# First modulation loaded by pairs of features, the gate columns multiplied behind the fourth tile

## What is computed

```python
c_act = silu(c)                                   # one row for the prompt, one for the sample
mod = c_act @ ada_w + ada_b                       # 6 x 1024 columns: sh1, sc1, gt1, sh2, sc2, gt2
hn = rmsnorm(x, norm1_g) * (1 + sc1) + sh1
proj = hn @ w_in                                  # split into pb, pc, ph, q, k, v, z, a, bb, ga, gb
g = -exp(a_log) * softplus(a + dt_bias)           # a, bb: 8 columns each, the gate columns
beta = sigmoid(bb)
# convolutions, gated delta rule, two mixers, residual with gt1, second norm, feed-forward, final norm
```

## Time and profile before

| | us |
|---|---|
| median of 3 runs | 1252.98 (1252.93 to 1253.11) |
| profiled execution | 1251.88 |
| its span, first to last instruction | 1250.2 |
| PE busy | 1225.0 (98%) |
| DVE busy | 670.6 (54%) |
| ACT busy | 449.1 (36%) |
| mean granted PE clock | 0.992 of full |

### The profile page before, as it was taken

The page is one execution under the profiler, slowest core; times in us unless marked ns, Lnnn a source line. Parts: engine busy times, 40 slices in busy tenths (PEclk is TensorE's granted clock), DMA queues, the critical chain, the costliest instruction groups (busy, mean ns, idle before and its releaser), DMA issues.

```text
span 1250.2 us, 27424 instructions
## 1 busy us (share of the span) xinstructions
PE 1225.0 (98%) x11560; PEld 1175.0 (94%) x11560; DVE 670.6 (54%) x904; ACT 449.1 (36%) x798; POOL 117.2 (9%) x255
## 2 busy tenths in 40 slices
PE   6999999999999999999999999999999999999997
PEld 4899999999999999999999999979999999999997
DVE  5586566455464555544967984464543343343334
ACT  4584434223232222324343333363332332232254
POOL 5021111201102011011110001000300000000000
PEclk8999999999999999999999999999999999999999
DMA  9932233212222122144864567422422322222212
GB/s 274 269 89 78 76 86 94 61 52 69 62 68 63 52 84 57 35 111 153 239 199 133 158 207 287 142 61 84 129 75 84 85 85 85 84 83 76 79 52 77
DMA packets 193886, 135.44 MB, mean 108 GB/s; under 512 B 4570, under 2 KB 185276, under 8 KB 192504
## 3 DMA queue, kind: packets, MB, share of 16 engines
q1 hardware_dynamic: 186320, 105.30, 30.0%
q0 software_dynamic: 7008, 28.48, 6.8%
q10 hardware_dynamic: 456, 0.16, 0.1%
HBM read 128.02 MB, written 5.90 MB: 107 GB/s over the span
## 4 chain that ended last, share of the span: by engine, by line
PE 93%; DVE 2%; SPq 2%; ACT 2%; DMA 1%; issue 0%; DVEq 0%; ACTq 0%
PE gp L575 79%; PE dp L779 2%; PE gp L601 2%; PE dp L788 1%; SPq L308 1%; PE dp L844 1%; PE dp L810 1%; PE dp L829 1%; PE dp L837 1%; PE dp L789 1%; PE dp L749 1%; PE dp L816 1%; DMA ada_w<-in_ada_w 1%; SPq L304 1%; PE dp L819 0%
## 5 line engine op out<-in xcount | busy, mean ns | idle before, releaser
L575 PE MATMUL gp<-a_hi,w_hi 128*128 128x288 f32 x1856 | 406.9, 301 | 2.3 <-DVE w_lo L1429 2.3
L575 PE MATMUL gp<-a_hi,w_lo 128*128 128x288 f32 x1856 | 397.3, 296 | 0.0
L575 PE MATMUL gp<-a_lo,w_hi 128*128 128x288 f32 x1856 | 396.9, 295 | 0.0
L575 PEld LDWEIGHTS gp<-a_hi,w_hi 128*128 128x128 f32 x1856 | 296.8, 189 | 13.1 <-issue 4.1
L575 PEld LDWEIGHTS gp<-a_hi,w_lo 128*128 128x128 f32 x1856 | 298.8, 189 | 0.0
L575 PEld LDWEIGHTS gp<-a_lo,w_hi 128*128 128x128 f32 x1856 | 298.3, 188 | 0.0
L1429 DVE TENSOR_TENSOR w_lo<-w_raw,w_hi 128x1024 fp32r<-128x1024 f32 x160 | 196.0, 1225 | 110.3 <-ACT w_hi L1023 109.3
L1184 ACT ACTIVATE xp<-gp 128x576 f32<-128x576 f32 x113 | 73.7, 652 | 452.5 <-PE gp L575 432.4
L1023 ACT ACTIVATE w_hi<-w_raw 128x1024 fp32r<-128x1024 f32 x160 | 168.8, 1055 | 2.3 <-DMA w_raw<-in_w_in 2.2
L575 PE MATMUL gp<-f_hi,w_hi 128*128 128x288 f32 x496 | 106.8, 297 | 0.0
L575 PE MATMUL gp<-f_lo,w_hi 128*128 128x288 f32 x496 | 106.2, 296 | 0.0
(11 more groups left out here) (314 smaller groups left out, 1258.0 us busy)
## 6 DMA issues: line engine op xcount, KB each, us to landing
w_raw<-in_w_in SPq DMA_DIRECT2D x72, 512.0 KB, 3.8
w_raw<-in_w_ff SPq DMA_DIRECT2D x64, 512.0 KB, 4.0
ada_half<-in_ada_w POOLq DMA_DIRECT2D x32, 512.0 KB, 4.6
ada_w<-in_ada_w SPq DMA_DIRECT2D x16, 512.0 KB, 7.5
w_raw<-in_w_a_out SPq DMA_DIRECT2D x8, 512.0 KB, 4.4
w_raw<-in_w_b_out SPq DMA_DIRECT2D x8, 512.0 KB, 4.1
w_raw<-in_w_o SPq DMA_DIRECT2D x8, 512.0 KB, 5.8
fin_vu<-in_final_ada_w POOLq DMA_DIRECT2D x4, 1024.0 KB, 18.6
```

The source lines that it names most:

```text
L575: last = T_.matmul(gp[:, 2 * b + h, 0:HALF], wp[:, b, k, :], ap[:, k, h * HALF:(h + 1) * HALF], start=(k == 0 and wp is w_hi and ap is hi) ...
```

## The change

- The weight of the first modulation comes in four blocks of 2 MB, each for two features: two DMAs of 1024 x 256 in rows of 1 KB. Row product, row copy and turn are made four times instead of eight, with twice the columns.
- The rows of c (c_p, c_s) are turned by themselves ahead of x; c_act is made behind the first x tile. Of the other rows, seven go by SP's queue behind block 0, four by ACT's.
- DVE scales four features before it copies the vectors; it splits the low part of tile 0 between the first pair's sample and low parts.
- PE's order is written out anew: tile 1 no longer runs four features behind tile 0 but close to it at the end.
- PE gets five filler products of ones and x (`keep_busy`): one before and one after row product 0, three behind turn 0.
- The gate columns are loaded last (POOL waits for block 3), high and low part side by side as 128 columns, and multiplied behind tile 3: 32 matmuls instead of 48. DVE adds the two halves. The gates are worked out beside tiles 4 to 7 instead of 0 to 3.

The diff, cut to its core:

```diff
 SP
-        for f in range(KT):
+        def ada_block(q):
             for e in range(2):
-                sp.dma_start(ada0_w[:, f, :, e, :], ada_v[:, :, D * e + f * P:D * e + f * P + P]).then_inc(ada_full[f], 16)
-            if f in (0, 2):
-                load(f // 2, 0, f // 2, wt(w_in, C_QKV + f // 2 * P))
+                sp.dma_start(ada0_w[:, q, :, 2 * P * e:2 * P * e + 2 * P], ada_v[:, :, D * e + 2 * P * q:D * e + 2 * P * q + 2 * P])\
+                    .then_inc(ada_full[q], 16)
+        ada_block(0)
+        row("ada_b", ...); row("cache_a", ...); row("conv_a_w", ...); row("final_g", ...)
+        row("out_g", ...); row("pad", ...); row("final_b", ...)
+        load(0, 0, 0, wt(w_in, C_QKV))
+        ada_block(1)
+        load(1, 0, 1, wt(w_in, C_QKV + P))
+        ada_block(2)
+        ada_block(3)
 POOL, behind its masks
+        pool.wait_ge(ada_full[3], 32)
+        ... the four DMAs of the gate columns and biases, moved here
 PE
-        def ada_first(f):
+        def ada_first(q):
...
-                last = T_.matmul(B0[32 * j:32 * j + 2, 0:2 * P], c_act[:, k, :],
-                                 ada0_w[:, f, k, :, :].rearrange("p e c -> p (e c)"), start=(k < 4), stop=(k >= 4))
+                last = T_.matmul(B0[32 * j:32 * j + 2, :], c_act[:, k, :], ada0_w[:, q, k, :], start=(k < 4), stop=(k >= 4))
-        def ada_turn(f):
+        def ada_turn(q):
...
+                pe.wait_ge(S["vecs_done"], 1)
+            for i in range(4):
+                last = T_.matmul(B3[:, 2 * i:2 * i + 2], mrow[:, i * P:(i + 1) * P], one4, start=True, stop=True)
+        def keep_busy(n):
+            for i in range(n):
+                T_.matmul(gp[:, 1, :], ones[:, :], xT[:, i % KT, 0:TP], start=True, stop=True)
         pe.wait_ge(S["consts"], 1)
+        pe.wait_ge(S["c_in"], 32)
+        T_.transpose(B2[:, 0:2 * KT], vrows[0:2 * KT, 0, :], ident[0:2 * KT, 0:2 * KT]).then_inc(S["c_t"], 1)
...
+        keep_busy(1)
         ada_first(0)
-        ada_first(1)
+        pe.wait_ge(S["rows_in"], 16 * 11)
+        ... the turn of the row vectors, moved here
+        keep_busy(1)
         ada_turn(0)
+        keep_busy(3)
-        two_products(0, a_hi, a_lo, "h_ready", 0, gate_rows, ahead=next_columns)
+        feature(0, 0)
+        ada_first(1)
+        feature(0, 1)
+        ada_turn(1)
+        feature(0, 2)
+        feature(1, 0, 3)
+        ada_first(2)
+        feature(0, 3)
+        ada_turn(2)
+        feature(1, 3)
+        feature(0, 4)
+        ada_first(3)
+        feature(1, 4)
+        ada_turn(3)
+        for k in range(5, KT):
+            feature(0, k)
+            feature(1, k)
         for n in (2, 3):
             products(n, n % 2, a_hi, a_lo)
+        gate_rows()
...
-                pe.wait_ge(S["row_a"], 1)
+                pe.wait_ge(S["ab_sum"], 1)
 ACT
         ada_row(0)
-        ada_row(1)
-        for f in range(KT):
-            act.wait_ge(S["mod_f"], f + 1)
-            modulated(0, 0, 0, f)
-            if f == 2:
+        w_split(0, 0, 0)
+        for q in range(4):
+            if q:
+                ada_row(q)
+            for f in (2 * q, 2 * q + 1):
+                act.wait_ge(S["mod_f"], f + 1)
+                modulated(0, 0, 0, f)
+            if q == 0:
                 w_split(1, 0, 1)
...
         for n in range(4, NQKV):
             qkv_in(n, n // 4, n % 4)
             qkv_out(...)
+            gates(n - 4)
 DVE
-        lo_split(0, 0)
         dve.wait_ge(S["rstd_done"], 1)
-        for f in range(2):
+        for f in range(4):
             scaled(rstd1, 0, f)
+        dve.wait_ge(S["vecs_t"], 1)
+        V_.tensor_copy(vecs[:, :], B3[:, 0:NVEC]).then_inc(S["vecs_done"], 1)
+        for q in range(4):
+            first_columns(q)
+            for f in (2 * q, 2 * q + 1):
+                sample(0, f)
+            if q == 0:
+                lo_split(0, 0)
+            for f in (2 * q, 2 * q + 1):
+                dve.wait_ge(S["hi_split"], f + 1)
+                TT(a_lo[:, f, :], norm_buf[f % 4], a_hi[:, f, :].bitcast(F32), ALU.subtract).then_inc(S["h_ready"], 1)
+            if q == 0:
                 lo_split(1, 1)
+            if q < 2:
+                for f in (2 * q + 4, 2 * q + 5):
+                    scaled(rstd1, 0, f)
...
-        for n in range(4):
-            conv(n, n)
-            gates(n)
+        for n in range(8):
+            conv(n, n % 4)
+            if n == 1:
+                ... the low part of the gate columns
+            if n >= 4:
+                gates(n - 4)
```

More of the change, by code:

```diff
@@ L445, in _ @@
         pool.memset(o_ss[:, 6:7], 0.0).then_inc(S["pool_ready"], 1)
+        pool.wait_ge(ada_full[3], 32)
+        v = w_in.rearrange("(k p) n -> p k n", p=P)
+        with nc.allow_non_contiguous_dma(reason="16 columns"):
+            pool.dma_start(ab_raw[:, :, 0:8], v[:, :, C_AB:C_AB + 8]).then_inc(S["ab_in"], 16)
+            pool.dma_start(ab_raw[:, :, 32:40], v[:, :, C_AB + 8:C_AB + 16]).then_inc(S["ab_in"], 16)
+            pool.dma_start(bias[0:H, 0:1], A["dt_bias"].rearrange("l h -> h l")).then_inc(S["ab_in"], 16)
+            pool.dma_start(bias[0:H, 1:2], A["a_log"].rearrange("l h -> h l")).then_inc(S["ab_in"], 16)
         c0, t0 = VEC["cache_qkv"][0], (WB - 1) * NQKV
@@ L644, in _ @@
                     last.then_inc(S["xt_ready"], 1)
[L645 to L649, removed]
         pe.wait_ge(S["xt_done"], 8)
@@ L654, in _ @@
         T_.matmul(gp[:, 3, 0:TS], ones[0:TS, :], diag1[0:TS, 4, 0:TS], start=True, stop=True).then_inc(S["rb_done"], 1)
+        keep_busy(1)
         ada_first(0)
-        ada_first(1)
+        pe.wait_ge(S["rows_in"], 16 * 11)
+        for g in range(3):
+            n = min(P, NVEC - g * P)
+            last = T_.transpose(B3[:, g * P:g * P + n], vrows[0:n, g, :], ident[0:n, 0:n])
+        last.then_inc(S["vecs_t"], 1)
+        keep_busy(1)
         ada_turn(0)
+        keep_busy(3)
         def ada_columns(bank, src, n):
@@ L663, in ada_columns, with feature, gate_rows @@
             last.then_inc(S["ada_t"], 1)
[L665 to L681, removed]
-        two_products(0, a_hi, a_lo, "h_ready", 0, gate_rows, ahead=next_columns)
+        def feature(n, k0, k1=None):
+            products(n, n, a_hi, a_lo, "h_ready", 0, k0, k1 or k0 + 1)
+        feature(0, 0)
[15 more added lines that the diff above has]
+            feature(1, k)
+        def gate_rows():
+            pe.wait_ge(S["ab_split"], 1)
+            for k in range(KT):
+                for ap in (a_hi, a_lo):
+                    for h, bank in enumerate((B1, B2)):
+                        last = T_.matmul(bank[:, 0:HALF], ab_both[:, k, :], ap[:, k, h * HALF:(h + 1) * HALF],
+                                         start=(k == 0 and ap is a_hi), stop=(k == KT - 1 and ap is a_lo))
+            last.then_inc(S["ab_ready"], 1)
         for n in (2, 3):
             products(n, n % 2, a_hi, a_lo)
+        gate_rows()
         def square_rows(q):
             if q == 0:
-                pe.wait_ge(S["row_a"], 1)
+                pe.wait_ge(S["ab_sum"], 1)
                 pe.wait_ge(S["one_done"], 2)
@@ L1043, in _ @@
         row("conv_qkv_w", A["conv_qkv_w"][0].rearrange("j (n p) -> (j n) p", p=P))
-        row("conv_a_w", A["conv_a_w"][0].rearrange("j (n p) -> (j n) p", p=P))
         row("norm1_g", A["norm1_g"].rearrange("l (n p) -> (l n) p", p=P))
+        row("norm2_g", A["norm2_g"].rearrange("l (n p) -> (l n) p", p=P))
         row("cache_qkv", A["cache_conv_qkv"][0, 0].rearrange("j (n p) -> (j n) p", p=P))
[L1047 to L1053, removed]
+        act.wait_ge(S["c_t"], 1)
+        AC(scales[:, 2].rearrange("p k g -> p (k g)"), B2[:, 0:2 * KT], ACT.Exp, scale=-1.0).then_inc(S["cexp_done"], 1)
         act.wait_ge(S["consts"], 2)
@@ L1085, in ada_rows, with ada_row @@
             AC(dst[:, :], bk[:, :], ACT.Copy).then_inc(S["ada_row_sb"], 1)
[L1087 to L1091, removed]
[L1092 to L1093 removed]
+        def ada_row(q):
+            act.wait_ge(S["ada0_used"], q + 1)
+            if q:
+                act.wait_ge(S["ada0_t"], q)
+            AC(mrow[:, :], B0, ACT.Copy).then_inc(S["ab0_row"], 1)
         def modulated(k, r, b0, f):
@@ L1509, in _ @@
         dve.wait_ge(S["rstd_done"], 1)
-        for f in range(2):
+        for f in range(4):
             scaled(rstd1, 0, f)
-        for f in range(KT):
-            first_columns(f)
-            sample(0, f)
-            if f + 2 < KT:
-                scaled(rstd1, 0, f + 2)
-            dve.wait_ge(S["hi_split"], f + 1)
-            TT(a_lo[:, f, :], norm_buf[f % 4], a_hi[:, f, :].bitcast(F32), ALU.subtract).then_inc(S["h_ready"], 1)
-            if f == 2:
+        dve.wait_ge(S["vecs_t"], 1)
@@ L1526, in gates @@
         def gates(part):
-            if part == 1:
+            if part == 0:
+                dve.wait_ge(S["ab_low"], 1)
+                TT(ab_sb[0:CH, 0:HALF], B1[0:CH, 0:HALF], ab_e[0:CH, 0:HALF], ALU.add)
```

(2 more changed lines are left out.)

119 lines of the change are left out of this document (59 added, 60 removed).

## The result

| | before | after |
|---|---|---|
| median, us | 1253.03 (4 runs, 1252.93 to 1253.11) | 1264.26 (4 runs, 1263.89 to 1265.14) |
| profiled execution, us | 1251.88 | 1264.42 |
| its span, us | 1250.2 | 1262.7 |
| PE busy, us | 1225.0 | 1229.0 |
| tile 4 starts, us | 73.50 | 82.19 |

The change makes the kernel slower: ratio 1.0092, 95% interval 1.008 to 1.0105, +11.2 us. The forecast was +4.5 with a range that ended at 1262; the sign was right and the size was not.

What follows compares the result with a forecast made beforehand. TensorE was taken as the bound, busy 1225.0 of 1250.2 us. A 2.0 us stall in the gate work plus 2.5 us at half clock gave +4.5 us, from 1252.98 to 1257.5 us, range 1251 to 1262.

Steps and rivals of the forecast that it cites:

- What bounds, and that a shift of the start goes through: Whole kernel: PE busy 1225.0 of 1250.2 us; after 73.5 us a start shift reaches the end one to one.
- Loads: Start: 1 KB rows move at about 340 GB/s; block 0 lands at 15.1 us, blocks 1 to 3 near 23.2, 31.2, 39.2.
- Start: Up to the first feature: DVE, not the load, sets block 0's chain; vectors end at 19.6 us, turn at 20.7.
- Blocks, tile 1's weight: ACT's copy of row product 1 queues behind tile 1's high half: costs nothing, 1 us with late loads.
- Blocks, PE's order: Features (0,2) and (1,0) to (1,2), 3.2 us, stand ahead of row product 2 though block 2 landed near 31 us.
- rival "faster": Modulation blocks overlap better than summed: three blocks end 5 us sooner, -3.0 us in all, 1250.0 us; chance 0.13.
- Clock: Behind the 3.6 us idle before feature (0,2): 5 us at half clock lose 2.5 us, bounds 1.3 and 5.1.
- The third rival: Clock falls a second time behind the 2.7 us wait before feature (0,4): +7.5 us, 1260.5 us; chance 0.17.
- Handover: From tiles 0 and 1 to tile 2: PE idles 2.3 us, so tile 2 starts at 56.5 us.
- gates: Gate columns behind tile 3: 32 matmuls at 0.133 us each take 4.3 us; tile 4 starts at 73.5 us as before.
- gate chain: Gate work moved beside tiles 4 to 7: PE stalls 2.0 us (0 to 3) before the square products behind tile 6.
- Sum: Whole kernel: +2.0 us at full clock plus 2.5 us for half clock make +4.5 us, a median of 1257.5 us.

## Why the prediction was right, and where it was wrong

- **What bounds, and that a shift of the start goes through.** Right: +10.7 us at the square products, the same distance through the middle, and the rest in the last products.
- **Loads.** The rate of 1 KB rows was right, 350 and 351 GB/s in the windows shown against 340. The landing of block 0 was not, 17.6 against 15.1, of which the move of x_sample's load takes away 0.9. PE waited 0.66 us for it; the loads behind it were late as well, tile 1's weight landing at 27.65 and not at 25.0. Block 3 was put at 39.2, but by the prediction's own figures it is 37.4, since no weight tile stands before it; it landed at 39.8, and PE never waited for it.
- **Start.** 25.65 against 24.2 for the first feature, within the doubt stated; c's rows cost next to nothing, as said. One link was misread: "row product 0 is done well before". It ran from 17.76 to 19.66, PE turned the row vectors behind it, and DVE's copy of them, forecast to end at 19.6, waited 0.44 us for that and ended at 20.8. The scalings before it were late as well, 19.9 for 19.1.
- **Blocks, tile 1's weight.** "Nothing, with late loads 1 us": the loads were late and the 1 us was about right, but it came on another engine. ACT's copy was hardly late; DVE stood behind the same weight. Its low half ended near 30.0, two scalings near 31.5, while turn 1 was done at 30.33. With the late first feature that made 2.5 us at feature (0,2); the run that moves the split takes 1.1 of them away.
- **Blocks, PE's order.** The prediction saw that features (0,2) and (1,0) to (1,2) stand ahead of product 2 although its block is there, and took 3.2 us for it. With the clock at half it was 6.13, and the start of it was late. It had set this against its rival "faster", and rightly: of the single edits only the changed order brings the kernel level with the one before (1254.17). With the clock held, the other order is worth 5.9 us, near the 5 us that this rival had named.
- **Clock.** This is the step that failed, by size. The mechanism was stated, and the wait of some 3.6 us before feature (0,2) was there (4.55). But the term was one fall, "5 us at half clock lose 2.5; bounds 1.3 and 5.1". The trace has three falls before tile 4, of 2.9, 1.5 and 1.8 us, 6.2 in all, and nine fillers in the waits bring tile 4 forward by 5.8. The third rival, a second fall before feature (0,4), came true, priced at 3 us; with it came one in tile 2 behind the handover, which the prediction had priced at the wait of 2.3 alone. The bare wait was priced in each case, the dense run behind it in the forecast only once. The first two falls come in all seven traces with this order and without the nine fillers. The one in tile 2 comes in two of the six with this handover, and whether it or the one in the last products, 1.6 us, comes is a matter of the execution.
- **Handover, gates, gate chain.** Right: 2.33 us against 2.3, 4.23 against 4.3, 1.8 against 2.0. Undoing the first and the last takes each wait off the path, by the landmarks.
- **Sum.** At full clock +2.0 was forecast; with fillers in the waits +4.6 was measured, and the 2.6 between are the late second pair. The remaining 6.7 are the clock, 5.8 of them before tile 4.

The Trainium skill, "TensorE: Matmul & The Clock Gate", section on HAM oscillation, describes a kernel whose short bursts each start cold behind a wait for a load. The windows behind 34.87 and 48.10 agree, at 0.50; the waits here were for VectorE.

## What to carry to other kernels

Price a new wait of TensorE as the wait and the half clock of the dense run behind it, for every wait of a chain and not for the worst one; where the engine waits for a load right after, the half clock cost at most 0.9 us here. In an order written out by hand, put work whose operands are there ahead of work that waits, even where that work is "next"; here that order alone was worth 10 us of 11. Filler products pay (2 us for the five of the change, some 6 for nine more) if they stand in waits ahead of dense work on the path, and brought nothing in the kernel before, where the loads set the pace.

## What the runs showed of the hardware

- The granted clock fell to 0.50 behind waits of 4.54, 2.60, 2.33 and even 0.75 us, and behind the shorter ones not each time: tiles 2 and 3 took 14.57 us in one kernel and 13.06 in another with the same instructions there, and behind the wait of 0.75 us it fell in six traces of thirteen. The Trainium skill says that the cold stretch at a kernel's start varies from run to run ("TensorE: Matmul & The Clock Gate", section What's actually happening); here the same is seen at the end of the kernel.
- Ten microseconds at half clock cost at most 0.9 us in the kernel before (ratio 1.0003 without them, 0.9993 to 1.0012). In the changed one the three stretches before tile 4 lost 6.2 us, and fillers gave 5.8 of them back at tile 4.
- While a load of 64 partitions was in flight, the rate of all loads together was 155 to 183 GB/s instead of about 350, with all DMA engines shown as busy. The Trainium skill, "DMA: Bandwidth & Descriptors", section The descriptor swizzle, has the lower 64 partitions written through half of the ports; that would fit, and no run here shows ports.
- Rows of 512 bytes moved at 292 GB/s, of 1 KB at 350.
